# State stores moved to SyncE's queue, and sample B and C rows spread by single-pass products

## What is computed

```
x, B, C   = silu(conv(...))                      # of the new position
dt        = softplus(dt_raw + dt_bias);  a = exp(dt * A)
new_state = a * state + (x * dt) outer B         # (8, 32, 64, 128), an output
y         = (C . state) * a + (C . B) * x * dt + d_skip * x
```

## Time and profile before

| what | us |
|---|---|
| three runs | 1102.05, 1098.62, 1093.25 |
| median | 1098.62 |
| profiled execution, its own time | 1096.22 |
| its span, first to last instruction | 1094.4 |
| TensorE busy in it | 1010.6 (92%) |
| VectorE, ScalarE, GpSimd busy | 701.6, 532.5, 246.8 |
| from the first product of spreading to the first of bs0 | 827.5 to 952.5 |

### The profile page before, as it was taken

One profiled execution on the slowest core, in us unless ns is written; L12 is line 12 of the kernel. 1 busy time (PEld: TensorE's weight loads), 2 busy tenths in 40 slices (PEclk: granted clock), 3 DMA queues, 4 the chain that ended last, 5 costly groups with the idle time before them and its releaser, 6 DMA issues.

```text
span 1094.4 us, 21697 instructions
## 1 busy us (share of the span) xinstructions
PE 1010.6 (92%) x8444; PEld 939.3 (86%) x8444; DVE 701.6 (64%) x1117; ACT 532.5 (49%) x1271; POOL 246.8 (23%) x327
## 2 busy tenths in 40 slices
PE   3999988898989899999999999999999998599998
PEld 2999888888989887469998998998999998599998
DVE  6857476564656559577887787887855566823432
ACT  5335555464645655125556456456445667412110
POOL 0222122222223101002202202202201988300000
PEclk9999999999999999999999999999999999799999
DMA  9542335236341037672472472472387997432221
GB/s 377 231 184 116 121 148 221 81 131 256 130 180 54 26 129 252 219 274 86 176 281 92 160 292 80 165 286 111 146 343 307 338 369 294 153 119 77 84 101 49
DMA packets 30261, 198.00 MB, mean 181 GB/s; under 512 B 4520, under 2 KB 6792, under 8 KB 20688
## 3 DMA queue, kind: packets, MB, share of 16 engines
q1 hardware_dynamic: 25664, 183.09, 44.1%
q0 software_dynamic: 4496, 13.54, 3.2%
HBM read 179.89 MB, written 104.70 MB: 260 GB/s over the span
## 4 chain that ended last, share of the span: by engine, by line
PE 60%; DVE 16%; ACT 14%; issue 7%; DMA 3%; SPq 0%; POOL 0%; DVEq 0%; ACTq 0%; POOLq 0%
PE bank L682 32%; PE bank L716 8%; PE bank L729 5%; ACT wH L1262 4%; DVE cacc L1677 4%; ACT Sx L1426 2%; DMA slot<-in_state_ssm 1%; DVE yL L2108 1%; PE bank L1000 1%; PE bank L982 1%; PE bank L905 1%; PE bank L805 1%; PE bank L974 1%; PE bank L845 1%; DVE Sx L1809 1%
## 5 line engine op out<-in xcount | busy, mean ns | idle before, releaser
L1656 DVE TENSOR_TENSOR wL<-w_raw,wH 128x2048 fp32r<-128x2048 f32 (+1 forms) x63 | 144.3, 2291 | 108.1 <-ACT wH L1262 106.1
L682 PE MATMUL bank<-xH,wH 128*128 128x260 f32 x976 | 203.6, 290 | 4.0 <-DVEq L1601 1.4
L682 PE MATMUL bank<-xH,wL 128*128 128x260 f32 x976 | 196.3, 283 | 0.0
L682 PE MATMUL bank<-xL,wH 128*128 128x260 f32 x976 | 195.8, 282 | 0.0
L1262 ACT CAST wH<-w_raw 128x2048 fp32r<-128x2048 f32 (+1 forms) x63 | 119.0, 1889 | 90.5 <-PE bank L682 82.4
L682 PEld LDWEIGHTS bank<-xH,wH 128*128 128x128 f32 x976 | 150.0, 188 | 13.6 <-issue 11.3
L716 PE MATMUL bank<-wH,xH 128*128 128x256 f32 x480 | 144.5, 301 | 18.0 <-DVEq L1601 11.0
L682 PEld LDWEIGHTS bank<-xL,wH 128*128 128x128 f32 x976 | 150.3, 188 | 0.0
L682 PEld LDWEIGHTS bank<-xH,wL 128*128 128x128 f32 x976 | 150.1, 188 | 0.0
L716 PE MATMUL bank<-wL,xH 128*128 128x256 f32 x480 | 138.9, 289 | 0.0
L716 PE MATMUL bank<-wH,xL 128*128 128x256 f32 x480 | 138.6, 289 | 0.0
(11 more groups left out here) (296 smaller groups left out, 2056.7 us busy)
## 6 DMA issues: line engine op xcount, KB each, us to landing
w_raw<-in_weights SPq DMA_DIRECT2D x62, 1024.0 KB, 5.1
out_kvs<-in_cache SPq DMA_DIRECT2D x16, 2044.0 KB, 10.5
ring<-in_cache SPq DMA_DIRECT2D x48, 256.0 KB, 4.0
slot<-in_state_ssm SPq DMA_DIRECT2D x16, 512.0 KB, 6.2
out_ssm_s<-slot POOLq DMA_DIRECT2D x16, 512.0 KB, 6.3
out_kvs<-in_cache SPq DMA_DIRECT2D x8, 508.0 KB, 7.0
out_kvp<-st POOLq DMA_DIRECT2D x18, 128.0 KB, 3.8
out_kvp<-vv POOLq DMA_DIRECT2D x18, 128.0 KB, 5.3
```

Source lines behind the costliest of these rows:

```text
L682: mm = pe.matmul(bk[hf].tile[:, 0:HALF], wslot(w, i)[:, k, s * P:(s + 1) * P], x[:, k, hf * HALF:(hf + 1) * HALF], start=(k == 0 and n == ...
L1656: TT(wL[:, i % 2, 0:k * n], raw[:, i % 2, 0:k * n], wH[:, i % 2, 0:k * n].bitcast(F32), ALU.subtract)\
```

## The change

Two edits.

**Stores.** GpSimd no longer issues the stores of the states. A new step `sstore` makes SyncE wait for `sample_state_ready` of unit u and issue the store, at beat u + 2. The reload of unit u moves from beat u + 2 to beat u - 2 and stands right behind the store of unit u - 4. Behind its add GpSimd now goes straight to the next `outer`, which waits for the add before.

**Spreading.** A new step `srows`, once, behind `sproducts`: TensorE turns all 64 columns of `BCS` in one transpose (bank 7), ScalarE copies the 64 rows as the high part, VectorE puts the low part in rows 64 to 127 of the same tile `rows2`, and builds `pick`, whose column r has a one in rows r and r + 64. Each of the 16 products of a group then takes a column of `pick`, repeated, as the stationary side and `rows2` as the moving side, both in the single-pass type.

```diff
-    out += [use, ("barrier",), ("sproducts",), ("oparts",)]
+    out += [use, ("barrier",), ("sproducts",), ("srows",), ("oparts",)]
...
-        if SLOTS_S <= beat - 2 < UNITS:
-            out.append(("sload", beat - 2))
+        if 0 <= beat - 2 < UNITS:
+            out.append(("sstore", beat - 2))
+            if SLOTS_S <= beat + SLOTS_S - 3 < UNITS:
+                out.append(("sload", beat + SLOTS_S - 3))
...
-    out += [("sload", UNITS - 1)] if len(rest) - 2 < UNITS else []
...
+                elif op == "srows":
+
+                    pe.wait_ge(S["bc_samples_kept"], GROUPS)
+                    banks[7].take(pe, ("rows",))
+                    pe.transpose(banks[7].tile[0:SROWS, 0:P], BCS[:, :, :, :].rearrange("p q g b -> p (q g b)"), ident)\
+                      .then_inc(banks[7].filled, 1)
...
-                                mm = pe.matmul(bk.tile[:, c * P:(c + 1) * P], BCS[:, q, g, b:b + 1].to_broadcast([P, P]), ident,
+                                r = (q * GROUPS + g) * B + b
+                                mm = pe.matmul(bk.tile[:, c * P:(c + 1) * P], pick[:, r:r + 1].to_broadcast([P, P]), rows2[:, :],
                                                start=True, stop=True)
...
+                elif op == "sstore":
+                    u = a[0]
+                    sp.wait_ge(S["sample_state_ready"], u + 1)
+                    sp.dma_start(ssms_out[u], slots[u % SLOTS_S][:, :, :]).then_inc(S[f"state_kept{u % SLOTS_S}"], 16)
...
+                    else:
+                        pool.wait_ge(S["sample_state_ready"], u)
...
-                    pool.wait_ge(S["sample_state_ready"], u + 1)
-                    pool.dma_start(ssms_out[u], st_u[:, :, :]).then_inc(S[f"state_kept{u % SLOTS_S}"], 16)
...
+                elif op == "srows":
+                    banks[7].full(act, ("rows",))
+                    cp(rows2[0:SROWS, :], banks[7].tile[0:SROWS, 0:P]).then_inc(S["sample_rows_ready"], 1)
...
+                elif op == "srows":
+                    TT(pick[:, :], con[:, C_ID:C_ID + SROWS], con[:, C_ID + SROWS:C_ID + 2 * SROWS], ALU.add)
+                    banks[7].full(dve, ("rows",))
+                    dve.wait_ge(S["sample_rows_ready"], 1)
+                    TT(rows2[SROWS:2 * SROWS, :], banks[7].tile[0:SROWS, 0:P], rows2[0:SROWS, :].bitcast(F32), ALU.subtract)\
+                        .then_inc(S["sample_rows_ready"], 1)
```

More of the change, by code:

```diff
@@ L532, in hybrid_kernel @@
         rs8 = a4.tile("rs8", [P, GROUPS, B])
+        SROWS = 2 * GROUPS * B
+        pick = a4.tile("pick", [P, SROWS], F32R)
+        rows2 = a4.tile("rows2", [P, P], F32R)
         yL = nc.alloc_sbuf_tensor_at("yL", [P, UNITS, R], F32R, offset=base)
@@ L554, in hybrid_kernel @@
             sample_exponents sample_exps sample_probs_turned
-            sample_q_ready sample_squares_ready sample_state_read
+            sample_q_ready sample_squares_ready sample_rows_ready sample_state_read
             sample_outer_ready sample_scale_ready sample_state_ready sample_xdt_ready sample_y_high_ready sample_y_low_ready sample_y_ready scaled_c_ready scaled_rows_ready
@@ L1010, in _ @@
                     if g == 0:
-                        pe.wait_ge(S["bc_samples_kept"], GROUPS)
+                        pe.wait_ge(S["sample_rows_ready"], 2)
                     for q, key in ((1, "Csp"), (0, "Bsp")):
@@ L2060, in _ @@
                     ins.then_inc(S["y_normed"], 1)
+                elif op == "srows":
[4 more added lines that the diff above has]
+                        .then_inc(S["sample_rows_ready"], 1)
+                    dve.wait_ge(S["sample_rows_ready"], 2)
+                    free(banks[7])
                 elif op == "oparts":
```

## The result

The changed kernel takes 1109.05 us (four runs, 1106.13 to 1113.62), the kernel before beside it 1097.88 (four runs, 1093.25 to 1102.05). The ratio is 1.0112, with a 95% interval from 1.0083 to 1.0142: slower by 11.2 us. The forecast was 1107, the range 1096 to 1116. The profiled execution of the changed kernel took 1107.99 us with a span of 1106.2, against 1096.22 and 1094.4 before: 11.8 us more.

The account below looks back on a forecast made before the run. TensorE, busy 92% of the span, was taken to bound the kernel, with the state-buffer loop reaching it. Late weight loads delay bs0 about 10.5 us, less 1.5; from median 1098.62 this gave 1107.6, stated as 1107, range 1096 to 1116.

Parts of the forecast that it names:

- 1: load of ga1 issued: SyncE's list: ga1's weight load waits behind store 0, issued 847.8 instead of 830.64, lands 854.3; no loss.
- 2: store 1 landed; load of ba0: SyncE's queue: store 1 lands behind the shift at 861.3, ba0's load follows at 861.8, its cast 5.0 us late.
- 3: load of ga2; third group: ga2's load waits behind add 4 and store 4; third group goes from 883.73 to 890.2, first loss TensorE feels.
- 4: load of ga3; fourth group: ga3's load waits behind add 8 and store 8; fourth group starts at 913.6 against 906.91, 6.7 us late.
- 6: load of bs0; read of unit 15; bs0: bs0's load waits behind add 12; VectorE reads unit 15 at 942.0, 10.5 us late, so bs0 starts about 10.5 late.
- The 1.5 us taken off: Discount on bs0's delay of about 10.5 us, because each leg was let begin only when the one before was whole.
- Step 5: ba1 lands 922.8, split 927.0; TensorE's products of beats 13 and 14 end 927.2, so no further loss.
- Alone this part is worth about 4 us: Shorter spreading products on TensorE: 0.3 to 0.7 us in the first group, 1.8 each in second and fourth.
- the ring: SyncE's weight loads wait for adds, adds for ScalarE's decays, decays for the previous weights' cast; bs0 about 10.5 us late.
- The clock rival: TensorE's granted clock falls behind the third group's longer wait, perhaps also ahead of bs0: up to 1114.6 us; chance 0.10.
- a TensorE that runs on at 0.64 behind 890: Sign named as showing the forecast wrong: TensorE's granted clock staying at 0.64 after 890 us.
- The other two rivals: SyncE's reloads and weights land in time, 1091 us, chance 0.16; or TensorE's products get no shorter, 1110 us, chance 0.08.

Follow-up runs that it names:

- the version with two edits: The changed kernel with weight loads one item earlier in SyncE's list and VectorE's cbd copy ahead of the split of gs3: 1092.93 us, 0.9962 of the kernel before.
- the run of the products with `cbd` first: Kernel before plus the new products only, with VectorE's copy cbd, which frees bank 6, ahead of the split of gs3: 1097.42 us, ratio 1.0000.

## Why the prediction was right

The number is 2.05 us under the measured one, and nearly by its own steps:

| step | predicted | profile after |
|---|---|---|
| 1: load of ga1 issued | 847.8 | 847.56 |
| 2: store 1 landed; load of ba0 | 861.3; 861.8 | 861.7; 862.10 |
| 3: load of ga2; third group | near 877; 890.2 | 877.45; 890.64 |
| 4: load of ga3; fourth group | near 901; 913.6 | 901.70; 914.55 |
| 5: ba1 landed; split | 922.8; 927.0 | 924.85; 929.2 |
| 6: load of bs0; read of unit 15; bs0 | near 932; 942.0; about 963.0 | 933.82; 944.12; 964.28 |

The casts of ba0, ga2 and ga3 wait for their weights, as said, and GpSimd issues nothing; a state costs it 4.52 us (outer at 896.43, the next at 900.95) for a predicted 4.45. A group takes 1.90 us for 1.84, above the two estimates that stood beside it (1.7 and 1.3). Taking the weight loads out from behind the stores gives 1097.63, which shows the cause, not only the sum.

Where it was wrong:

**The 1.5 us taken off.** The sum of the chain was +10.5, and bs0 came 11.8 us later, the median 11.2. The discount ("since I let each leg begin only when the one before is whole") had no row behind it. Without it the number would have been 1109 for 1109.05, and that would have been partly luck: the chain came out 1.3 us short, and the median that it was added to, 1098.62, lies 0.7 us above the 1097.88 measured beside the change. The ends have the same fault: ten per cent of the rate, 3.6 us, about a sum of 9 gives +5.4 to +12.6, not the +4 to +15 of the text.

**Step 5, "no further loss".** ba1 landed 2.0 us later than worked out and its split ended at 929.2 instead of 927.0. TensorE ended beat 14 at 928.1 and then waited 3.40 us, for a bank, not for the split. The bank is freed by ScalarE's instruction on the product before it:

```profile
924.88 1.91 ACT L1277 CAST wH<-w_raw 128x2048 fp32r<-128x2048 f32 x1 [7.17 <-DMA w_raw<-in_weights]
...
928.09 2.45 ACT L1593 ACTIVATE slot<-slot,dsb 128x128 f32<-128x128 f32 x8
930.44 0.86 ACT L1375 ACTIVATE mix<-bank 128x260 f32<-128x260 f32 x2
```

The cast came late, and the copies and the decays behind it had to go first. I compared the end of the split with the end of the products and left out what else stands behind the late cast on ScalarE. It did not change the end: VectorE's read of unit 15 sets bs0, and TensorE's 9.06 us ahead of 948.08 covers the 3.40 us.

**"Alone this part is worth about 4 us".** The term was mis-sized. Alone it gave nothing (1.0015). The 0.3 to 0.7 us of the first group was a loss, by the wait of 2.38 us and the clock behind it; the 1.8 of the fourth went in part into the longer wait ahead of it. With the first group mended it is worth 2.6 to 2.7 us. In the forecast this hardly showed, since the ring, and not the products, set the end.

**The clock rival, given 0.10.** Its mechanism came and its price did not. The clock fell behind the long wait at the third group, as it said: 0.50 over 890 to 895 and 0.72 over the next 5 us. The prediction had named a TensorE that runs on at 0.64 behind 890 as a sign against itself, and that sign came, for 10 us. Over the whole stage the low clock cost TensorE 6.7 us of busy time. But the fourth group starts when VectorE has read unit 11, and TensorE was there 1.26 us before, at half clock or not. The rival put 4.4 of its 6 us under that wait; it was all of them. Ahead of bs0 the wait stayed at 3.49 us, with the clock at 1.00 behind it.

The other two rivals fell: the ring had no slack, and a group takes 1.9 us, not 3.6. The page on DMA of the Trainium skill ("DMA: Bandwidth & Descriptors", "SWDGE vs HWDGE vs iDMA") calls the setup of descriptors made in hardware the faster one. The traces show no such gain: a store from SyncE landed in 3.0 us where nothing was ahead of it (876.59), and one from GpSimd in the kernel before in 2.9 us (939.75). The 5.83 us of the earlier trace rows were not the price of GpSimd's queue. Behind a shift, SyncE's store took 10.0 us (851.67). What a store stands behind matters more here than who makes its descriptors.

## What to carry to other kernels

An engine that only issues transfers is a list like any other. Moving an instruction with a late wait into it delays every transfer behind it; if one of these feeds the engines that the wait is for, the delay closes into a ring and comes back at each turn. Before such a move, write out that list with its waits, put first what is needed soonest and waits for least, and then follow every transfer behind each wait, on the second edit too: the same reordering of the weight loads gave 11.4 us with early reloads and cost 21 with late ones. Shorter products gave 2.6 to 2.7 of 7 us here, since TensorE then waited longer for the engines that free its banks; so look first at who the next wait is for.

## What the hardware showed that I had not expected

**The clock behind short waits.** With the old products a wait of 1.31 us in the first group left the granted clock at 1.00; with half as many products in front and a wait of 2.38 us it fell to 0.57 over the next 4 us. It was 1.00 again once the first group had no wait in it. At the start of bs0 it is one or the other behind nearly the same wait. It is 1.00 in the kernel before behind 3.47 us, and in the changed kernel behind 3.49 us,

```profile
964.30:969.30 5.00, 5.00 (x42) 5.00 (x43) 2.29 (x1) 0.62 (x1) 0.00 (x0) 1.00 0.86 356
```

but in the version with two edits, behind 3.45 us,

```profile
947.50:952.50 5.00, 5.00 (x29) 5.00 (x30) 2.29 (x1) 0.62 (x1) 0.00 (x0) 0.66 0.87 364
```

and in the same version with the old products, behind 3.37 us,

```profile
951.00:956.00 5.00, 5.00 (x23) 5.00 (x24) 2.29 (x1) 0.62 (x1) 0.00 (x0) 0.50 0.84 356
```

it is lower, by the work of 1.7 and 2.5 us. The traces of the other nine kernels have 0.50 to 0.69 there, behind waits of 1.9 to 4.9 us; the two of the kernels before and after are the exceptions of thirteen. There is one trace for each kernel, so whether the same kernel goes both ways at this place is not shown. Its executions do differ as a whole: among 35 of the kernel before the mean clock goes from 0.989 (1093.95 us) to 0.980 (1102.04 us). So a single trace, which differs by some 2 us at this one place alone, cannot price what the products are worth; the medians of many runs were needed.

**VectorE's splits and GpSimd's instructions take turns.** In the run of the products with `cbd` first, a split of 2.29 us took 4.49 (875.17) beside GpSimd's outer of 1.90 us (875.60), and the add behind that took 4.30 instead of 2.40 (877.57). Four parts took 5.0 to 6.3 us beside GpSimd and 2.50 without, in the kernels before and after. VectorE's reads of the states, with one input from a bank, kept their 1.29 us (868.36, beside GpSimd's outer at 868.96). The prediction priced this for the parts and for an outer behind a split, not for a split behind GpSimd. In the changed kernel it made no difference, since there all splits of the stage took 2.28 or 2.29 us.
